# First phase of a decoder block: x loaded by one queue, six w_ada units summed by TensorE, and the order of loads and splits around them

## What is computed

```python
c_act = jax.nn.silu(c)
mod = (c_act @ w_ada[l] + b_ada[l])[:, None, :]          # 1 x 2048 times 2048 x 12288
shift_m, scale_m, gate_m, shift_f, scale_f, gate_f = jnp.split(mod, 6, axis=-1)
h = rmsnorm(x, g_pre_mix[l]) * (1 + scale_m) + shift_m   # 256 x 2048
z = h @ w_in[l]                                          # the first large product
```

## Time and profile before

| | |
|---|---|
| median of 3 runs | 1590.75 us (1590.11 to 1590.86) |
| the profiled execution's own time | 1588.88 us |
| its span | 1587.1 us |
| TensorE busy | 1567.0 us (99%) |
| VectorE busy | 1120.1 us (71%) |
| ScalarE busy | 821.0 us (52%) |

### The profile page before, as it was taken

How to read it: one execution, slowest core, us unless ns; L and a number is a source line. 1 busy time by engine, 2 the same in 40 slices (tenths; PEclk the granted TensorE clock), 3 DMA queues, 4 the chain that set the end, 5 groups by cost and what they waited for, 6 DMA issues and landing times.

```text
span 1587.1 us, 29303 instructions
## 1 busy us (share of the span) xinstructions
PE 1567.0 (99%) x11685; PEld 1482.7 (93%) x11685; DVE 1120.1 (71%) x1277; ACT 821.0 (52%) x1076; POOL 6.5 (0%) x12
## 2 busy tenths in 40 slices
PE   7999999999999999999999999999999999999998
PEld 7999999889999999999789999999999999888886
DVE  5897877987867785877757777777777665544444
ACT  5567776657634634434446555455454454444342
POOL 0000000000000000000000000000000000000000
PEclk9999999999999999999999999999999999999999
DMA  9999988884488887877964777777776565555553
GB/s 370 351 320 350 323 269 259 304 274 147 146 277 278 296 280 252 288 262 262 330 208 126 246 239 243 236 240 238 243 251 215 187 198 198 198 199 186 192 197 139
DMA packets 190650, 389.51 MB, mean 245 GB/s; under 512 B 18386, under 2 KB 31058, under 8 KB 189794
## 3 DMA queue, kind: packets, MB, share of 16 engines
q1 hardware_dynamic: 185666, 370.40, 69.4%
q10 hardware_dynamic: 4898, 17.90, 3.3%
HBM read 386.16 MB, written 2.10 MB: 245 GB/s over the span
## 4 chain that ended last, share of the span: by engine, by line
PE 95%; DVE 2%; ACT 1%; issue 1%; DMA 0%; DVEq 0%; ACTq 0%
PE ps L592 21%; PE ps L596 20%; PE ps L594 20%; PE ps L619 8%; PE ps L621 8%; PE ps L620 8%; PE ps L794 1%; PE ps L542 1%; DVE w_lo L1416 1%; PE ps L565 1%; DMA x_tok<-in_x 0%; PE ps L695 0%; PE ps L703 0%; PE ps L816 0%; PE ps L669 0%
## 5 line engine op out<-in xcount | busy, mean ns | idle before, releaser
L1416 DVE TENSOR_TENSOR w_lo<-raw,w_hi 128x1024 fp32r<-128x1024 f32 x530 | 625.8, 1221 | 410.4 <-ACT w_hi L997 409.6
L997 ACT ACTIVATE w_hi<-raw 128x1024 fp32r<-128x1024 f32 x530 | 533.0, 1052 | 626.1 <-PE ps L596 407.2
L592 PE MATMUL ps<-h2t,w_hi 128*128 128x256 f32 x1408 | 389.9, 277 | 0.7 <-DVE h2t L1844 0.7
L594 PE MATMUL ps<-h2t,w_hi 128*128 128x256 f32 x1408 | 388.7, 276 | 0.0
L596 PE MATMUL ps<-h2t,w_lo 128*128 128x256 f32 x1408 | 388.7, 276 | 0.0
L592 PE MATMUL ps<-ht,w_hi 128*128 128x256 f32 x1104 | 309.5, 280 | 0.0
L594 PE MATMUL ps<-ht,w_hi 128*128 128x256 f32 x1104 | 305.5, 277 | 0.0
L596 PE MATMUL ps<-ht,w_lo 128*128 128x256 f32 x1104 | 305.5, 277 | 0.0
L592 PEld LDWEIGHTS ps<-h2t,w_hi 128*128 128x128 f32 x1408 | 264.3, 188 | 0.9 <-issue 0.9
L594 PEld LDWEIGHTS ps<-h2t,w_hi 128*128 128x128 f32 x1408 | 264.4, 188 | 0.0
L596 PEld LDWEIGHTS ps<-h2t,w_lo 128*128 128x128 f32 x1408 | 264.3, 188 | 0.0
(11 more groups left out here) (284 smaller groups left out, 1999.2 us busy)
## 6 DMA issues: line engine op xcount, KB each, us to landing
raw<-in_w_ffn_up SPq DMA_DIRECT2D x176, 512.0 KB, 4.5
raw<-in_w_in SPq DMA_DIRECT2D x168, 512.0 KB, 5.1
ada<-in_w_ada SPq DMA_DIRECT2D x148, 512.0 KB, 6.6
raw<-in_w_ffn_down SPq DMA_DIRECT2D x88, 512.0 KB, 4.0
raw<-in_w_branch_b SPq DMA_DIRECT2D x32, 512.0 KB, 5.4
raw<-in_w_mix_out SPq DMA_DIRECT2D x32, 512.0 KB, 5.2
ada<-in_w_ada ACTq DMA_DIRECT2D x32, 512.0 KB, 4.0
raw<-in_w_branch_a SPq DMA_DIRECT2D x16, 512.0 KB, 5.4
```

Of the source, the lines that this page charges most:

```text
L592: mm(o, w_hi[:, s, k, cols], moving[:, kt, 0], start=opens, stop=False, skip_group_check=True)
L594: mm(o, w_hi[:, s, k, cols], moving[:, kt, 1], start=False, stop=False, skip_group_check=True)
L997: A(w_hi[:, slot], raw[:, slot], ACT.Copy).then_inc(hi_done, 1)
L1416: V.tensor_tensor(w_lo[:, slot], raw[:, slot], w_hi[:, slot].bitcast(F32), ALU.subtract)\
```

## The change

SP issues both tiles of x, in turn, ahead of the w_ada units. Units 1, 2 and 14 are summed by TensorE as well (units 1 and 2 before the transposes, unit 14 ahead of `half_columns` of half 1), and the waits with `busy(2)` and `busy(3)` go; the last `busy(6)` becomes `busy(8)`. `FIRST_HALF`, 10 in place of 14, counts VectorE's products in half 0. VectorE makes `h_f` for half 0, and ScalarE writes the hi part of h between its first and second split. VectorE does splits 1 and 2 ahead of all units of half 1, and split 3 after `take_first_mod` of half 1. The loads of `rows`, `pos_i` and `masks_i` are issued in the loop at k = 1, behind the two units of pair 3.

```diff
--- before.py
+++ after.py
@@ -104,7 +104,8 @@
 
 UNITS = 2 * len(PAIRS)
 FIRST_PASSES = 3
-ON_TENSOR = (6, 8, 9)
+ON_TENSOR = (1, 2, 6, 8, 9, 14)
+FIRST_HALF = 2 * sum(a not in ON_TENSOR for a in range(8))
 LAT = at_pair("qlat", 0, 12)
 MLA = at_pair("gk", 1, 8)
 GLA = MLA + 11
@@ -453,7 +454,7 @@
                 r = a % RING
                 loaded = ada_loaded[r]
                 if a < KT + RING:
-                    sp.wait_ge(half_used, 14 + 2 * (a - KT + 1))
+                    sp.wait_ge(half_used, FIRST_HALF + 2 * (a - KT + 1))
                 else:
                     sp.wait_ge(ada_used, a - (RING - 1))
                 if a < 2 * ADA_BLOCK:
@@ -465,7 +466,8 @@
                     sp.dma_start(ada[:, r], w_ada[kt * P:(kt + 1) * P, c0:c0 + AC]).then_inc(loaded, 16)
 
             sp.dma_start(fixed[:], const_f).then_inc(const_loaded, 16)
-            sp.dma_start(x_tok[:, 1], x[0, P:2 * P, :]).then_inc(x_loaded[1], 16)
+            for t in range(NT):
+                sp.dma_start(x_tok[:, t], x[0, t * P:(t + 1) * P, :]).then_inc(x_loaded[t], 16)
             for a in range(8):
                 load_half_ada(a)
             for u in range(FIRST_PASSES):
@@ -474,13 +476,14 @@
                 load_half_ada(a)
             for u in range(FIRST_PASSES, 2 * FIRST_PASSES):
                 load_first(u)
-            sp.dma_start(pos_i[:], positions[0:1, :].to_broadcast([P, S])).then_inc(pos_loaded, 16)
-            sp.dma_start(rows[:, 1:5], all_rows[:, 1:5]).then_inc(rows_loaded, 16)
-            sp.dma_start(masks_i[:, :, :].rearrange("p l n -> p (l n)"), const_m).then_inc(masks_loaded, 16)
 
             for k in range(FFN):
                 if FIRST_PASSES <= k + 2 < FFN:
                     load_pair(k + 2)
+                if k == 1:
+                    sp.dma_start(rows[:, 1:5], all_rows[:, 1:5]).then_inc(rows_loaded, 16)
+                    sp.dma_start(pos_i[:], positions[0:1, :].to_broadcast([P, S])).then_inc(pos_loaded, 16)
+                    sp.dma_start(masks_i[:, :, :].rearrange("p l n -> p (l n)"), const_m).then_inc(masks_loaded, 16)
                 for n in range(ADA_AT[k]):
                     load_ada(ADA_BEFORE[k] + n)
                 if k == MLA + 9:
@@ -832,6 +835,8 @@
             nc.tensor.transpose(ps[:, 7, 0:P], rows[:, 0, :], ident[:]).then_inc(rows_t, 1)
             pe.wait_ge(c_ready, 1)
             busy(20, 7)
+            tensor_ada(1, True)
+            tensor_ada(2, False)
             for b in range(8):
                 if b % 4 == 0:
                     pe.wait_ge(norm_x, 2 * (b // 4 + 1))
@@ -842,11 +847,8 @@
                     ins = nc.tensor.transpose(ps[:, b % 6, q * P:(q + 1) * P], xn_tok[:, t, kt * P:(kt + 1) * P], ident[:])
                 ins.then_inc(xt_psum, 1)
             pe.wait_ge(setup_done, 2)
-            tensor_ada(6, True)
-            for n in range(11, 14):
-                pe.wait_ge(half_used, n)
-                busy(2, 7)
-            pe.wait_ge(half_used, 14)
+            tensor_ada(6, False)
+            pe.wait_ge(half_used, FIRST_HALF)
             half_columns(0, 0, False)
             busy(7, 7)
             first_unit(0)
@@ -854,12 +856,10 @@
             first_unit(1)
             tensor_ada(9, False)
             first_unit(2)
-            for n in range(24, 26):
-                pe.wait_ge(half_used, n)
-                busy(3, 6)
+            tensor_ada(14, False)
             pe.wait_ge(ada_used, KT)
             half_columns(0, 1, False)
-            busy(6, 6)
+            busy(8, 6)
             for u in range(FIRST_PASSES, 2 * FIRST_PASSES):
                 first_unit(u)
             pe.wait_ge(mod_ready, 2)
@@ -1054,7 +1054,6 @@
                     seed(START[i][0] + b, home(kind, g, b))
 
             nc.scalar.dma_start(rows[:, 0], all_rows[:, 0]).then_inc(first_rows_loaded, 16)
-            nc.scalar.dma_start(x_tok[:, 0], x[0, 0:P, :]).then_inc(x_loaded[0], 16)
             nc.scalar.preload_act_table(ACT.Silu)
             act.wait_ge(rows_t, 1)
             own.mark(A(vec[:, 0:P], ps[:, 7, 0:P], ACT.Copy))
@@ -1160,13 +1159,9 @@
                     act.wait_ge(og_summed, hd)
                 A(o_sq[:], o_gla[:, 4 * hd:4 * hd + 4], ACT.Square).then_inc(og_squared, 1)
 
-            for u in range(2):
-                split(u, u, total[u], None, 0)
+            split(0, 0, total[0], None, 0)
             input_hi(0, 0)
-            for kt in range(2):
-                ins = A(h_f[:, kt], xn_t[:, kt], ACT.Identity, bias=mod[:, 0, kt:kt + 1], scale=mod[:, 1, kt:kt + 1])
-            ins.then_inc(h_ready, 1)
-            for u in range(2, RING):
+            for u in range(1, RING):
                 split(u, u, total[u], None, 0)
             input_hi(0, 1)
 
@@ -1690,15 +1685,15 @@
                     half_ada(a)
             take_first_mod(0, 0)
             split(0, 0)
+            input_f(0, 0)
             input_lo(0, 0)
             split(1, 1)
-            half_ada(10)
-            half_ada(11)
             split(2, 2)
-            for a in range(12, 16):
-                half_ada(a)
+            for a in range(8, 16):
+                if a not in ON_TENSOR:
+                    half_ada(a)
+            take_first_mod(0, 1)
             split(3, 3)
-            take_first_mod(0, 1)
             input_f(0, 1)
             input_lo(0, 1)
```

## The result

The changed kernel takes 1592.2 us in the median of 20 runs, the kernel before 1589.27 us in 20 runs beside them; the ratio is 1.0016, with an interval of 1.0009 to 1.0023. By the medians it is slower by 2.9 us, by the ratio by some 2.6 us, where 2.2 us less were forecast. The three runs of the kernel before that the forecast started from are among these 20 and lie high in them (1590.75 against 1589.27).

A forecast was written before the change was run, and what follows sets the result against it. Bound: a TensorE queue behind the first phase, so pair k = 3's earlier start counts. Terms -0.8 -1.45 +0.34 +0.1 = -1.8 us, or -3.3 with half the transposes at full clock; -2.2 taken: 1588.55 us, range 1586.4 to 1591.0.

The forecast's parts named there:

- Small loads later: Small loads behind w_in units 6 and 7: rows lands at 46.0 us, units 8 and 9 at 50.5 and 51.9, no stall.
- cover 2.9 us: Before pair k = 4: unit 9 lands at 51.9 us, wanted at 54.8 for the two splits.
- units 8 and 9 are late: No-change rival, chance 0.15: the 1.8 us gained at 42 us are given back to loads; 1590.4 to 1590.8 us.
- the slow rival: Chance 0.06: rows lands late, at 55.6 us, and stops TensorE before the L869 transposes; +2.8 us, 1593.5.
- busy taken out of half 0: -1.45: Before the columns of half 0: removing busy takes 1.45 us off the chain; unit 6 ends at 23.2, VectorE's sum at 21.2.
- w_ada unit 7: In half 0: the load lands at 19.6 us, VectorE's sum ends at 21.2 and is not on the path.
- a sign of being wrong: At either columns: the prediction is wrong if VectorE's sum and not TensorE is last.
- The sum: Start of the first phase through busy(8): -0.8 -1.45 +0.34 +0.1 = -1.8 us, with transposes wholly at half clock.
- the first rival: Chance 0.15: the clock stays up over units 1 and 2 and the transposes; -3.8 us, 1586.9.
- Unit 14: +0.34: In half 1: unit 14 on TensorE takes 1.68 us where 1.34 us of busy stood, +0.34 us.

The follow-up runs named there:

- e1: Changed kernel with the three small loads (rows, pos_i, masks_i) issued ahead of the loop again; 1589.92 us, ratio 1.0002 to the kernel before.
- e2: Changed kernel with VectorE's split 3 ahead of take_first_mod of half 1 again, small loads still late; 1589.04 us, ratio 1.0000 to the kernel before.
- m2: Changed kernel with split 3 ahead of take_first_mod and the one-column products near 382 us divided into two groups; 1588.21 us.
- r1: Changed kernel with only the one-column products near 382 us divided into two groups; 1591.24 us, ratio 1.0006 to the kernel before.
- m4: Kernel before with the one-column products near 382 us divided and without the five groups of busy between waits; 1587.99 us.
- e4: Kernel before with only the three small loads moved to k = 1 behind pair 3; 1589.39 us, ratio 0.9996 to the kernel before.
- m1: Kernel before with only the one-column products near 382 us divided into two groups, take_mod one pair later; 1588.09 us, ratio 0.9995.
- x1: m1 with only x issued by SP, in turn; 1587.17 us, ratio 0.9986 to the kernel before.
- r2_look: The kernel of r1, unchanged, profiled once more; 1590.21 us in that profile.
- b2: m3 with unit 14 on VectorE again; 1586.49 us, ratio 0.9982 to the kernel before.
- m3: m2 with small loads early and two busy(2) ahead of the columns of half 0, each behind one more VectorE product; 1587.30 us, ratio 0.9991.

## Why the prediction was wrong, step by step

**The step that failed: "Small loads later", "cover 2.9 us".** It added 1.35 us per unit from 37.21 us on, as if the queue were full throughout and transfers alone set the pace, and so let unit 7 land at 45.3 and unit 9 at 51.9 us. But SP could issue unit 7 only at 43.28 us, when the DMA engines had been all but idle for over a microsecond, had then to issue all the rest one by one, and unit 9's last piece, issued at 49.70, landed at 56.84: 4.9 us later than forecast. The text had both facts, that unit 7 waits for split 3 and that split 3 now follows `mod`, and counted neither the issues behind it nor the time from issue to landing, which it allowed for `rows` alone. Those 7.1 us are not special to units in pieces: the whole w_in units issued from 40 to 58 us took 8.0 in the median. The cost is 1.3 to 2.0 us of TensorE's wait, in two of six profiles over a microsecond more by the clock. By the medians it is 2.3 and 3.2 us between e1 or e2 and the changed kernel, and 3.0 us between m2 and r1, which differ in split 3 alone but ran in different series (1.9 us by their ratios). The rival that named this ("units 8 and 9 are late") had 0.15 and was priced as taking back the gain, not more; the slow rival named `rows`, for which nothing waited.

**"busy taken out of half 0: -1.45".** The fills had hidden nothing in an ordinary run of the kernel before, where VectorE's sum at 23.1 to 23.5 us is next (m4: 0.1 us). And without them, with units 1, 2 and 6 on TensorE, the clock falls in two thirds of the profiles, for 1.5 us in `busy(7)`. The prediction also says that the sums behind both pieces of `busy` were ready; that holds for half 0 only. In half 1 VectorE's sum ended at 41.12 us, 0.8 us after TensorE's first units:

```profile
37.87 3.25 DVE L1454 SCALAR_TENSOR_TENSOR acc<-ada_next,c_act,acc 128x512 f32<-128x512 f32 x4
```

**w_ada unit 7.** Forecast at 19.6 us, it landed at 20.91. VectorE's sum ended at 22.5 us in place of 21.2 and was last at the first columns, which the prediction had named as a sign of being wrong. That the columns still ended near the forecast is in part luck: the transposes took 5.4 us and not 6.6, so TensorE was through with unit 6 at 22.2 and not at 23.2 us, which made room for a sum that came 1.3 us late. In four of the nine profiles without a fill unit 7 was there at 19.7 to 19.8 us, as forecast.

**The base line.** The 53.17 us of k = 3 in the earlier trace rows contain transposes wholly at half clock. Other profiles with the order of before have 51.4 (e4), 51.5 (m1) and 51.3 (m4, in spite of a shorter fall in the transposes). The sum took 1.8 us off a draw that was itself 1.7 us worse than those; against them the changed kernel's 52.23 us are later and not sooner.

**Right.** Transposes began at 15.20 us (14.9 forecast), with the clock at 0.5 in a part of them; columns of half 0 ended at 23.66 (24.0, see above). x in turn does what was said: alone, in x1, it lets the transposes begin at 13.88 us (13.9). k = 3 was 0.94 us sooner in the profile, 1.8 forecast. That the one-column products of units 1 and 2 don't keep the clock was right as a tendency: it fell between 14 and 17 us in nine of the twelve profiles with these units on TensorE (in two of the five with the idle stretch of before), and stayed up there in those of e1, r1 and r2_look. The prediction took one stretch, at 841 us, as its ground; the same 32 instructions at 382 us in the same profile had no fall. In r1 and r2_look nothing fell near 23 us either, w_ada unit 7 was early, and k = 3 came at 49.8 and 50.0 us, 3.3 and 3.2 us before, where the first rival had 3.8. The Trainium skill ("TensorE: Matmul & The Clock Gate", section "Why this matters for your kernels") speaks of idle gaps between bursts; the falls at 385 us and near 841 us show that a stretch without a gap can do the same.

**"Unit 14: +0.34".** At the spot it took its 1.68 us. VectorE, however, had 4.3 us to spare there: b2, which differs from m3 in unit 14 alone, is 0.8 us faster in the median (in another series) and 0.8 us sooner at k = 3.

**The account.** Of the 2.9 us between the medians, 2.3 to 3.2 are the loads. The rest of the change, without them, is worth nothing within the intervals (e1, e2, m2 against m1). x in turn is 0.9 us to the good (x1 against m1, in different series), so units 1, 2 and 14 and the removed fills together must give about that back; this is a difference and was not run by itself. How this second part divides among its edits was not measured apart, except for unit 14. The fp32 h on VectorE and the hi part ahead of split 1 were not tried alone; no profile shows a wait for them. The fall at 385 us, which is most of the difference between the two profiles shown first, is hardly an effect of the change: e4 has it with the order of before, and dividing the columns lowers the kernel before by 0.85 us and the changed kernel by 1.0 (r1, in another series).

## What to carry to other kernels

When an edit delays the instruction that frees a buffer, list every load that the issuing engine has queued behind that buffer, and count for the last of them the wait for the buffer, every issue in between and the time from issue to landing, not the transfers alone. Here two moves, each harmless alone, together made one load late. Before a gain is read off a chain, look at what comes second on it in other runs too; a fill that lies on the chain in one profile may stand in front of a sum that is only 0.1 us behind it in another. And where a profile contains a half-clock stretch, take several profiles of the kernel before as the base line.

## What the hardware showed

A run of 32 one-column instructions on TensorE, 3.6 us without a gap at full clock, was followed by a granted clock of 0.5 in five of six profiles near 382 us and in seventeen of seventeen near 841 us; divided into 16 and 16 with full products between, in none of eleven. 16 of them, followed by a short wait and 8 more, were followed by it in six of nine profiles behind units 1 and 2, and not in m4's, without them. A wait of 1.7 to 2.0 us at pair k = 4 was followed by the same in two of three profiles, one of 1.3 or 1.4 us in none of three. And SP needed 6.1 to 7.3 us in the six stalled profiles to issue what stood from w_in unit 7 to the last piece of unit 9, which then took 6.4 to 8.0 us to land.
